# A two-block transformer kernel on one core: fifth expert block's w1 and w3 loaded ahead of the third's w2, norms by tile, row additions on GpSimd, half-head transfers issued by SyncE and GpSimd

## The reference

```python
# first block
h = rms_norm(x, attn_norm)
x = x + hybrid_mixer(h, ...)                 # fox attention and sliding-window attention
h = rms_norm(x, ffn_norm)
x = x + hier_moe(h, ..., w1, w3, w2)         # 64 experts, 2 per token
x = rms_norm(x, final_norm)
# an expert block: (silu(xb @ w1[e]) * (xb @ w3[e])) @ w2[e]
# second block
xn = rmsnorm(h, pre_mix_norm)
mix = token_mixer(xn, ...)                   # retention (4 heads) and latent attention (8 heads), @ w_o
h = h + rmsnorm(mix, post_mix_norm)
hn = rmsnorm(h, pre_ffn_norm)
ff = (silu(hn @ w_gate) * (hn @ w_up)) @ w_down
h = h + rmsnorm(ff, post_ffn_norm)
e = rmsnorm(p @ w_ple_proj, ple_norm)
gate = sigmoid(h @ w_ple_gate + b_ple_gate)
h = h + e * gate
```

## Time and profile before

| | us |
|---|---|
| median of 3 runs | 2105.07 |
| lowest, highest | 2104.47, 2105.32 |
| the profiled execution | 2102.4 |
| its span | 2100.6 |
| TensorE busy (share of the span) | 1799.4 (86%) |
| VectorE busy | 778.0 (37%) |
| ScalarE busy | 694.8 (33%) |
| GpSimd busy | 77.6 (4%) |
| mean DMA rate | 241 GB/s |

### The profile page before, as it was taken

How to read it: one execution, slowest core, us unless ns; L and a number is a source line. 1 busy time by engine, 2 the same in 40 slices (tenths; PEclk the granted TensorE clock), 3 DMA queues, 4 the chain that set the end, 5 groups by cost and what they waited for, 6 DMA issues and landing times.

```text
span 2100.6 us, 35691 instructions
## 1 busy us (share of the span) xinstructions
PE 1799.4 (86%) x14374; PEld 1252.6 (60%) x14374; DVE 778.0 (37%) x1481; ACT 694.8 (33%) x1292; POOL 77.6 (4%) x184
## 2 busy tenths in 40 slices
PE   7999999787777778777777778699989899999988
PEld 5777787544444434344444444388667688788866
DVE  4555335632222222222222222444455533332254
ACT  4444422232222232222222232433555422222151
POOL 0000000000000000000000002410000000000000
PEclk9999999899999999999999999899989999999999
DMA  6222223689999999999999999742221232324211
GB/s 203 76 81 81 61 100 103 286 362 425 425 427 425 427 425 428 425 427 426 426 427 425 428 425 428 280 121 75 67 86 51 66 95 83 112 87 141 100 60 41
DMA packets 108457, 506.04 MB, mean 241 GB/s; under 512 B 9401, under 2 KB 58809, under 8 KB 75105
## 3 DMA queue, kind: packets, MB, share of 16 engines
q1 hardware_dynamic: 99888, 491.01, 58.5%
q10 hardware_dynamic: 7376, 10.84, 1.9%
q0 software_dynamic: 1120, 3.16, 0.5%
HBM read 497.31 MB, written 2.11 MB: 238 GB/s over the span
## 4 chain that ended last, share of the span: by engine, by line
PE 58%; DMA 29%; DVE 7%; ACT 3%; issue 2%; SPq 1%; ACTq 0%; DVEq 0%
DMA ring<-in_w 28%; PE bank L611 13%; PE bank L612 12%; PE bank L613 12%; PE bank L2155 8%; PE bank L2067 3%; PE bank L2146 3%; PE bank L775 2%; DVE w_lo L709 2%; ACT w_hi L696 1%; PE bank L801 1%; PE bank L787 1%; SPq L1718 1%; DMA raw<-in_w_in 1%; PE bank L1098 0%
## 5 line engine op out<-in xcount | busy, mean ns | idle before, releaser
L2155 PE MATMUL bank<-ring,XTs 128*32 128x256 f32 x4032 | 284.8, 427 | 115.8 <-DMA ring<-in_w 112.9
L2408 DVE TENSOR_TENSOR x<-x,bank 128x512 f32<-128x512 f32 x264 | 163.8, 681 | 486.4 <-PE bank L2146 486.4
L2155 PEld LDWEIGHTS bank<-ring,XTs 128*32 128x32 f32 x4032 | 154.2, 120 | 248.8 <-issue 187.8
L611 PE MATMUL bank<-hTh,w_hi 128*128 128x512 f32 x714 | 288.1, 404 | 13.5 <-DVE hTl L739 6.3
L709 DVE TENSOR_TENSOR w_lo<-raw,w_hi 128x2048 fp32r<-128x2048 f32 (+3 forms) x85 | 183.1, 2158 | 299.1 <-ACT w_hi L696 298.9
L612 PE MATMUL bank<-hTh,w_lo 128*128 128x512 f32 x714 | 283.6, 397 | 0.0
L613 PE MATMUL bank<-hTl,w_hi 128*128 128x512 f32 x714 | 281.2, 394 | 0.0
L696 ACT ACTIVATE w_hi<-raw 128x2048 fp32r<-128x2048 f32 (+3 forms) x85 | 152.8, 1804 | 173.3 <-PE bank L613 170.4
L2164 PE MATMUL bank<-ring,aT 128*32 128x256 f32 x2048 | 124.9, 383 | 90.1 <-DVE aT L2428 90.1
L1942 ACT ACTIVATE y<-bank 32x256 f32<-32x256 f32 x256 | 96.1, 376 | 227.0 <-PE bank L2146 140.7
L611 PEld LDWEIGHTS bank<-hTh,w_hi 128*128 128x128 f32 x714 | 135.8, 190 | 55.3 <-DVE w_lo L709 17.5
(11 more groups left out here) (377 smaller groups left out, 2256.9 us busy)
## 6 DMA issues: line engine op xcount, KB each, us to landing
ring<-in_w SPq DMA_DIRECT2D x190, 2048.0 KB, 19.6
raw<-in_w_in SPq DMA_DIRECT2D x25, 1024.0 KB, 5.5
raw<-in_w_gate SPq DMA_DIRECT2D x11, 1024.0 KB, 5.4
raw<-in_w_up SPq DMA_DIRECT2D x11, 1024.0 KB, 5.3
raw<-in_w_down SPq DMA_DIRECT2D x11, 1024.0 KB, 4.8
raw<-in_w_out SPq DMA_DIRECT2D x4, 1024.0 KB, 5.0
third<-in_w SPq DMA_DIRECT2D x2, 2048.0 KB, 22.8
raw<-in_w_o SPq DMA_DIRECT2D x4, 1024.0 KB, 5.2
```

What stands on the lines that cost most here:

```text
L611: pe.matmul(dst, left[0], right[0], start=start, stop=False)
L2155: mm = pe.matmul(Hb[BLK * j:BLK * (j + 1), :], XTs[u][:, 4 * (c % 2) + 2 * h + c // 2, :], w[:, at_:at_ + Q], start=(h == 0 and c == 0), s ...
L2408: ins = v.tensor_tensor(xs, xs, Sb[t % 2][n][:, :], ALU.add)
```

## The change

- SyncE issues w1 and w3 of expert 4 as soon as `w_used` is 2, ahead of w2 of expert 2 and all of expert 3's.
- Between the blocks ScalarE writes the square of x into `xg`, VectorE multiplies it by the squared gain (`gain_sq`, made by GpSimd) and sums, both norms' factor is formed per tile in `rstd2`, and ScalarE scales x itself into `xn4`. The gain of the final norm goes into the splits (`mix_gain`, the product of two columns). GpSimd multiplies x by the gain afterwards and scales it.
- The half-head transfers of the latent attention are issued by GpSimd (keys, lower half of the queries) and SyncE (upper half), the key rows by GpSimd; VectorE makes `w_lo` of `ukv` and the first retention products before it turns queries; two of ScalarE's key copies come earlier, the value copies go to VectorE; one unit less is split ahead of attention on VectorE.
- In the tail the norm `n7` is taken by tile (`TileNorm`), GpSimd adds the rows to x, half of `ple` is done after the transposes of `hT5`, the norm `n8` comes later, and `gated` comes one tile behind the bias in both halves.

The diff, cut to its core:

```diff
@@ SyncE, before the loop
+            sp.wait_ge(w_used, 2)
+            for m in range(2):
+                load_matrix(0, m, 4)
             sp.wait_ge(w_used, 4)
             load_matrix(0, 2, 2)
             for m, done in enumerate((2, 2, 4)):
                 sp.wait_ge(w_used, STEPS + done)
                 load_matrix(1, m, 3)
-
-            for m in range(2):
-                load_matrix(0, m, 4)
             sp.wait_ge(w_used, 2 * STEPS + 4)
@@ SyncE, loads of the second block
             for n in range(n_first + RAW, len(order)):
                 load(n)
+                if n == units_of["or1"][0].n:
+                    for k in range(2):
+                        read(sp, J["mq_r"][k:k + 1])
+                        swap(sp, f"mq_swapped{k}", mq_swap[k], mq_r[k], 64, P, 16)
@@ ScalarE, between the blocks
+            def rows_out(i):
+                act.wait_ge(S("tile_means"), n34 + i + 1)
+                chain(act.activation(rstd2[:, i:i + 1], rstd2[:, i:i + 1], ACT.Sqrt))
+                act.sem_inc(S("tile_roots"), 1)
+                act.wait_ge(S("n34"), i + 1)
+                act.activation(xn4(i), x[:, i, :], ACT.Copy, scale=rstd2[:, i:i + 1]).then_inc(S("xn4"), 1)
+
             for i in range(NT):
                 act.wait_ge(S("x2pre"), i + 1)
-                chain(act.activation(av(9216, D), x[:, i, :], ACT.Square, accum_out=ssq[:, i:i + 1]))
-                act.wait_ge(S("xg"), i + 1)
-                chain(act.activation(av(9216, D), xg(i), ACT.Square, accum_out=ssq2[:, i:i + 1]))
-            act.sem_inc(S("norm_squares"), 2)
+                act.activation(xg(i), x[:, i, :], ACT.Square, accum_out=ssq[:, i:i + 1]).then_inc(S("tile_squares"), 1)
+                if i >= 2:
+                    rows_out(i - 2)
+            rows_out(NT - 2)
+            rows_out(NT - 1)
...
@@ VectorE, between the blocks
+            def both_norms(i):
...
+                chain(v.tensor_tensor_reduce(xg(i), xg(i), gain_sq, 1.0, 0.0, ALU.mult, ALU.add, ssq2[:, one]))
+                chain(v.tensor_scalar(nsum[:, one], ssq[:, one], EPS / D, EPS * EPS, ALU.mult, ALU.add))
+                v.scalar_tensor_tensor(rstd2[:, one], ssq2[:, one], 1.0 / D, nsum[:, one], ALU.mult,
+                                       ALU.add).then_inc(S("tile_means"), 1)
...
             for t in range(NT):
                 flush(count + 1, t)
                 v.wait_ge(flushed, 4 * count + (t + 11))
                 v.sem_inc(S("x2pre"), 1)
-                v.tensor_tensor(xg(t), x[:, t, :], gain_fin, ALU.mult).then_inc(S("xg"), 1)
+            for i in range(NT):
+                both_norms(i)
+                if i:
+                    inverse(i - 1)
+            inverse(NT - 1)
+            v.tensor_scalar(rstd, ssq, 1.0 / D, EPS, ALU.mult, ALU.add).then_inc(S("norm_means"), 1)
             lo_until(v, n_first)
...
@@ GpSimd
+            pool.wait_ge(S("w_fin"), 16)
+            pool.tensor_tensor(gain_sq, gain_fin, gain_fin, ALU.mult).then_inc(S("gain_sq"), 1)
...
+            for i in range(NT):
+                chain(pool.tensor_tensor(xg(i), x[:, i, :], gain_fin, ALU.mult))
+                pool.tensor_scalar(x[:, i, :], xg(i), rstd[:, i:i + 1], None, ALU.mult).then_inc(S("x2"), 1)
+
+            read(pool, J["kr"])
+            swap(pool, "swapped", kr_swap, krot, ML_N, ML_QK, 16)
...
+            read(pool, J["mq_r"][0:1])
+            swap(pool, "swapped", mq_swap[0], mq_r[0], 0, 64, 16)
+            spread(0)
+            read(pool, J["mq_r"][1:2])
+            swap(pool, "swapped", mq_swap[1], mq_r[1], 0, 64, 16)
+            read(pool, J["ret_b"])
+            pool.wait_ge(S("kr_roped"), 1)
+            key_rows(0)
+            pool.wait_ge(S("ret_out"), RH)
+            key_rows(1)
+            spread(1)
+
             for i in range(NT):
-                pool.tensor_scalar(x[:, i, :], xg(i), rstd[:, i:i + 1], None, ALU.mult).then_inc(S("x2"), 1)
-            for k in range(2):
-                spread(k)
+                pool.wait_ge(S("ffn_rows"), i + 1)
+                pool.tensor_tensor(x[:, i, :], x[:, i, :], ffo[:, i, :], ALU.add).then_inc(S("x4"), 1)
@@ VectorE, mixer
-            turned(0)
-            v.wait_ge(S("kr_swapped"), 32)
-            k1, k2_ = ...
-            dve_rope(v, chain, k1, k2_, ...).then_inc(S("kr_roped"), 1)
             lo_until(v, units_of["ukv"][0].n)
             for h in range(RH):
                 job = J["ret_b"][h]
                 full(v, job)
                 free(v.tensor_tensor(rqT[:, h, :], rqT[:, h, :], banks[job.bank][:, :], ALU.mult), job)
-                read(v, [job])
+            turned(0)
+            k1, k2_ = ...
+            dve_rope(v, chain, k1, k2_, ...).then_inc(S("kr_roped"), 1)
+            read(v, J["ret_b"])
+            for h in range(RH):
                 v.scalar_tensor_tensor(rqT[:, h, :], rqT[:, h, :], PRM("ret_gn", h), rgT[:, h, :], ALU.mult,
                                        ALU.mult).then_inc(S("ret_f"), 1)
...
             turned(1)
+            for i, job in enumerate(J["mv"]):
+                full(v, job)
+                free(v.tensor_copy(mv[:, i, :], banks[job.bank][:, :]), job)
             lo_until(v, units_of["or0"][0].n)
-            lo_until(v, units_of["or1"][0].n)
@@ ScalarE, mixer
             queries(1)
+            hi_until(act, units_of["or0"][0].n)
+            read(act, J["ret_b"])
+            two_heads(J["mk"][0], mkT[0], 0, 1.0)
+            two_heads(J["mk"][1], mkT[0], 1, 1.0)
 
             for h in range(RH):
                 act.wait_ge(S("ret_f"), h + 1)
                 act_split(act, ("ret", h), osTh[:, h, :], rqT[:, h, :])
             two_heads(J["mq_n"][2], mqT, 2, -(ML_QK ** -0.5))
             two_heads(J["mq_n"][3], mqT, 3, -(ML_QK ** -0.5))
-            read(act, J["ret_b"])
-            act.wait_ge(S("kr_roped"), 1)
-            key_rows(0)
-            two_heads(J["mk"][0], mkT[0], 0, 1.0)
-            two_heads(J["mk"][1], mkT[0], 1, 1.0)
             act.wait_ge(S("ret_out"), RH)
-            key_rows(1)
...
@@ VectorE, tail
+            second_half(0)
+            for i in range(1, NT):
+                second_half(i)
+                if i == NT - 1:
+                    dve_split_jobs(v, "pT", *pT)
+                rows_added(i - 1)
+            rows_added(NT - 1)
+            lo_until(v, units_of["pg0"][0].n)
+            dve_split_jobs(v, "hT5", *hT5)
+            lo_until(v, units_of["pg0"][1].n)
             dve_rstd(v, chain, "n8", ssq2, rstd2, NT, D)
...
+            for n in range(2):
                 ahead(lo_until, v, f"pg{n}")
-                if n:
-                    gated(k - NT)
-                full(v, job)
                 cols = slice(512 * n, 512 * (n + 1))
-                v.tensor_tensor(pg_out[:, i, cols], banks[job.bank][:, :], bias_ple[:, cols], ALU.add).then_inc(S("pg"), 1)
-            for k in range(NT, 2 * NT):
-                gated(k)
+                for i, job in enumerate(J[f"pg{n}"]):
+                    full(v, job)
+                    v.tensor_tensor(pg_out[:, i, cols], banks[job.bank][:, :], bias_ple[:, cols], ALU.add).then_inc(S("pg"), 1)
+                    if i:
+                        gated(NT * n + i - 1)
+                gated(NT * n + NT - 1)
@@ TensorE, tail
+            ple(0)
+            pe.wait_ge(S("x4"), NT)
+            pe_to_feature(pe, J["hT5"], lambda i, c: x[:, i, P * c:P * (c + 1)])
+            ple(1)
```

168 lines of the change are left out of this document (91 added, 77 removed).

## The result

The changed kernel took 2080.87 us (median of 4 runs, 2079.52 to 2083.36), the kernel before 2104.77 in the same comparison (4 runs, 2104.09 to 2105.32). The ratio is 0.9888, 95% interval 0.9871 to 0.9905: 23.9 us faster. The prediction was 2079.3, range 2070 to 2092. The profiled execution of the changed kernel took 2081.62 us, its span is 2079.8, 20.8 less than before's 2100.6. Its first hidden product began 1.8 us later than before's (410.61 against 408.83), in code that wasn't changed. So each stage is measured from its own start.

The account below looks back on a forecast made before the run. Expert weight transfers at 426 GB/s bound 436 to 1320 us, TensorE the rest. Gains 9.0 + 2.5 + 6.5 + 7.8 = 25.8 off the profiled 2102.4 give 2076.6; 2.7 for the median makes 2079.3, range 2070 to 2092.

Parts of the forecast that it names:

- Part 1: Expert weight loads: issuing expert 4's w1 and w3 9.0 us earlier fills a stream hole; gain 9.0, ends 3 and 12.6.
- The walk: Hand schedule of weight loads, 4.9 us per matrix, 1.8 to start into an empty queue: expert 6's pair lands at 482.2.
- Part 2: Norms between the blocks: less work on VectorE and ScalarE shortens TensorE's 11.4 us idle; gain 2.5, ends 0 and 4.
- Part 3: Half-head transfers in the mixer: moving their issue removes TensorE's 4.41 us stall; gain 6.5, ends 3 and 9.5.
- Part 4: Tail: norm per tile, additions on GpSimd, half of `ple` over the splits; gain 7.8, ends 3.5 and 10.
- by the row it is 2029.7, which I take: Tail: GpSimd's last addition ends at 2029.7, as a VectorE subtract beside GpSimd's scalings still took 2.28 us.
- an addition over 3.4 us: Tail: sign that the forecast is wrong, if GpSimd's additions take more than 3.4 us each.
- By the rule: Tail: VectorE norm and GpSimd addition alternate, 1.28 + 2.6 per tile; GpSimd ends at about 2032.3, some 2.6 us later.
- (b): GpSimd and VectorE wait for each other and the low clock stays: gains sum to 18, 2087 us; chance 0.10.
- (a): Weight stream: the hole is only moved, to 453.8, so the load order brings 3; sum 19.8, 2085 us; chance 0.11.
- (c): Weight queue runs dry in each of 29 remaining pairs, 29 us lost against 25.8 gained: 2108 us; chance 0.06.
- (d): Load order brings nothing, since the second `w_used` isn't what holds the two places: 16.8 left, 2088 us; chance 0.04.

Follow-up runs that it names:

- e2_order_only: Changed kernel with expert 4's w1 and w3 still ahead of 2's w2, but all three issued only after `w_used` 4: 2084.03 us, ratio 0.9892.
- u1_order: Changed kernel with the old load order, expert 4's w1 and w3 behind expert 3's three: 2087.25 us, ratio 0.9916 to the kernel before.

## Why the prediction was right

The total, 2079.3 against 2080.87, is closer than its terms were: 9.0, 2.5, 6.5 and 7.8 were forecast, 5.9, 3.8, 7.7 and 5.0 are in the trace. Two terms too high and two too low: the misses are 3.1 and 2.8 one way, 1.3 and 1.2 the other. Such a close total is in part luck.

- **Part 1, 9.0 forecast, 5.9 measured.** The walk's shape was right: two loads 6.2 us behind the hidden product (5.8 forecast), dips where the queue held little, none after 490. (Its sign "no second under 400 GB/s from 417 to 430", where a microsecond is meant, wasn't met to the letter: single ones moved 328 GB/s, at 419, and 369, at 428.) The step that failed is "6's pair ... land at 482.2. In the trace they land at 491.15. Gain 9.0": it takes a walk from a trace. The same walk done for the kernel before, from 431.22 with 1.8 to start, eleven matrices of 4.92 and the row's 1.2, gives 488.3, so it runs 2.8 us ahead of the trace. For the changed kernel it gave 482.2 and the trace, less the 1.8 us of the late start, has 485.1: 2.9 ahead. Walk against walk is 6.1, and the trace has 6.0. e2_order_only, forecast this way, came out within 0.4.
- **Part 2, 2.5 forecast, 3.8 measured** (4.0 by its undoing). The tiles were forecast at 1353.5, 1356.3, 1358.3 and 1359.8. Shifted by the 4.09 us between the two traces they came at 1353.8, 1356.4, 1358.0 and 1359.5. The multiply with a sum took 1.20 to 1.23, and 1.3 was taken. Two things were mis-sized. VectorE's weight subtract began at what is 1358.3 in before's time, and the forecast needs 1359.2 (1361.5 less 2.28), so the first split came 0.9 sooner. And the deduction of 0.4 for slow first matmuls wasn't due: the first matmul took 0.47 us and the next 0.40, as before. The clock of the bursts was mostly the lower level, 0.57 in the mean from 1350 to 1355, but that lay in TensorE's waits for the tiles.
- **Part 3, 6.5 forecast, 7.7 measured.** No stall ahead of `ukv`, a stall of 2.2 in the values (2.9 forecast), the first output matmul at what is 1539.95 in before's time (1540.5 forecast). The deduction for the clock was right in this execution, where eight matmuls ahead of the first output matmul took 0.56 to 0.63 us; without it, as in three later ones, the gain is 9.4, the forecast's upper end of 9.5.
- **Part 4, 7.8 forecast, 5.0 measured** (5.3 by its undoing). The stall in `pg1` (1.94, forecast 2.0) and the end behind the last matmul (2076.05 + 0.69 - 2073.39 = 3.35, forecast 3.4) were right. The step that failed is "by the row it is 2029.7, which I take": GpSimd's last addition ended at 2016.98 + 15.77 = 2032.75 in before's time. The row that I trusted was a subtract that began at 1369.70, 0.21 us ahead of GpSimd's fourth scaling, so it showed the one that goes first and not the one that waits. The price that I needed was GpSimd's, and its four scalings stood merged in one row of 13.26 us. Taken apart they are three of 2.85 us and the fourth, so the trace of the kernel before already held the answer:

```profile
1369.91 4.79 POOL L2538 TENSOR_SCALAR x<-arena,small 128x1024 f32<-128x1024 f32 x1
```

  The prediction's own sign, an addition over 3.4 us, came true for one of the four (4.36). By the rule the sum gave 2032.3 and a part of 5.2, 0.45 us from the trace. The rule of the Trainium skill ("SBUF — State Buffer", "Who interferes with whom"), that the two exclude each other, agrees with the trace. That the sum came so close is in part luck: it took 2.6 us for an addition that takes 2.40, and 1.96 of the delay is the weight subtract ahead of the fourth addition, which neither sum names.

Of the rivals, (b) described the tail, but not parts 2 and 3; (a) was wrong in its mechanism, since the later dips are about as large as in the walk (1.3 and 2.2 us of stream against 1.1 and 2.7), and right in part of its size. (c) and (d) fell: 426 GB/s without a hole from 490 on, and u1_order 6.4 us slower. The range held because its ends came from bounds of each part.

## What to carry to other kernels

Take a walk only from a walk: do the hand schedule for the kernel before too, and price the change by the difference, since what the walk leaves out stands in both. Work moved from VectorE to GpSimd beside VectorE instructions with two SBUF inputs isn't parallel: put it beside splits and copies from PSUM, or leave it. Before trusting a row for a pair of engines, look at the one that began second, and take merged rows apart. And a subtract or copy without a deadline belongs behind whatever the other engine is waited for, ahead of what waits for a third engine: two such swaps took 3.7 us off this kernel's tail.
